# A three-layer fp32 block on one core: the order of work at its norm transitions, its first loads, and its filler matmuls are changed

## The reference, cut to what matters

```
h = rms_norm(x); proj = h @ w_in                 # first layer: retention and a gated recurrence
x = x + mix @ w_out                              # "out"
h = rms_norm(x); up = h @ w_up                   # norm transition 0, feed-forward 1 (conv, gelu, product)
x = rms_norm(x + hidden @ w_down)                # norm_f
for l in range(2):                               # two layers of a second kind
    h = swiglu_ffn(rms_norm(x)); x = x + 0.5 * rms_norm(h)       # feed-forward A
    h = hybrid_mixer(rms_norm(x)); x = x + rms_norm(h)           # mixer
    h = swiglu_ffn(rms_norm(x)); x = x + 0.5 * rms_norm(h)       # feed-forward B
```

## Time and profile before

| | |
|---|---|
| median of 3 runs | 1520.59 us (1520.00 to 1520.68) |
| the profiled execution | 1520.84 us |
| its span in the trace | 1518.7 us |
| PE busy | 1482.9 us, 98% of the span |
| DVE busy, ACT busy | 970.2 us (64%), 712.4 us (47%) |
| granted TensorE clock, mean | 0.999 of full speed |
| first product of a weight unit begins | 19.26 us |

### The profile page before, as it was taken

One profiled execution on the slowest core, in us unless ns is written; L12 is line 12 of the kernel. 1 busy time (PEld: TensorE's weight loads), 2 busy tenths in 40 slices (PEclk: granted clock), 3 DMA queues, 4 the chain that ended last, 5 costly groups with the idle time before them and its releaser, 6 DMA issues. The chain is left out here.

```text
span 1518.7 us, 21963 instructions
## 1 busy us (share of the span) xinstructions
PE 1482.9 (98%) x9232; PEld 1300.2 (86%) x9232; DVE 970.2 (64%) x1195; ACT 712.4 (47%) x878; POOL 39.5 (3%) x50
## 2 busy tenths in 40 slices
PE   7999999999999999999999999999999999999998
PEld 6999999899988788888987888878888899878886
DVE  5767786587864656545876666456664568666644
ACT  4533863455543544445245444444444444454432
POOL 0000000000000000001010000000000010000000
PEclk9999999999999999999999999999999999999999
DMA  7635465566655566465323755547655543366542
GB/s 245 222 121 167 141 198 189 159 189 180 182 194 166 180 221 210 151 196 139 112 98 112 228 182 185 188 145 228 229 194 168 139 123 115 102 192 192 194 148 101
DMA packets 253461, 259.17 MB, mean 171 GB/s; under 512 B 26659, under 2 KB 217524, under 8 KB 253364
## 3 DMA queue, kind: packets, MB, share of 16 engines
q1 hardware_dynamic: 251424, 254.44, 52.8%
q10 hardware_dynamic: 1940, 3.33, 0.6%
HBM read 256.69 MB, written 1.05 MB: 170 GB/s over the span
## 5 line engine op out<-in xcount | busy, mean ns | idle before, releaser
L971 DVE TENSOR_TENSOR w_lo<-raw,w_hi 128x2048 fp32r<-128x2048 f32 (+1 forms) x240 | 545.3, 2274 | 335.7 <-ACT w_hi L589 335.5
L589 ACT ACTIVATE w_hi<-raw 128x2048 fp32r<-128x2048 f32 (+1 forms) x240 | 455.9, 1900 | 345.3 <-PE stream L1634 145.4
L1634 PE MATMUL stream<-a_hi,w_hi 128*128 128x256 f32 x1072 | 306.4, 286 | 4.3 <-DVE a_lo L1008 3.2
L1634 PE MATMUL stream<-a_lo,w_hi 128*128 128x256 f32 x1072 | 303.3, 283 | 0.0
L1634 PE MATMUL stream<-a_hi,w_lo 128*128 128x256 f32 x1072 | 303.2, 283 | 0.0
L1634 PE MATMUL stream<-w_hi,a_hi 128*128 128x512 f32 (+1 forms) x640 | 244.0, 381 | 6.4 <-DVE w_lo L971 6.4
L1634 PE MATMUL stream<-w_hi,a_lo 128*128 128x512 f32 (+1 forms) x640 | 239.3, 374 | 0.0
L1634 PE MATMUL stream<-w_lo,a_hi 128*128 128x512 f32 (+1 forms) x640 | 238.9, 373 | 0.0
L1634 PEld LDWEIGHTS stream<-a_hi,w_hi 128*128 128x128 f32 x1072 | 205.6, 192 | 7.5 <-DVE w_lo L971 3.9
L1634 PEld LDWEIGHTS stream<-a_lo,w_hi 128*128 128x128 f32 x1072 | 205.7, 192 | 0.0
L1634 PEld LDWEIGHTS stream<-a_hi,w_lo 128*128 128x128 f32 x1072 | 205.6, 192 | 0.0
(11 more groups left out here) (282 smaller groups left out, 1612.0 us busy)
## 6 DMA issues: line engine op xcount, KB each, us to landing
raw<-in_ffn_w_up SPq DMA_DIRECT2D x136, 512.0 KB, 5.0
raw<-in_ffn_w_down SPq DMA_DIRECT2D x104, 512.0 KB, 4.5
raw<-in_ffn_w_gate SPq DMA_DIRECT2D x88, 512.0 KB, 3.9
raw<-in_w_in SPq DMA_DIRECT2D x78, 512.0 KB, 4.6
raw<-in_w_out SPq DMA_DIRECT2D x24, 512.0 KB, 4.2
raw<-in_w_ret_o SPq DMA_DIRECT2D x8, 512.0 KB, 4.1
raw<-in_w_lru_o SPq DMA_DIRECT2D x8, 512.0 KB, 4.0
diag<-in_conv_diag SPq DMA_DIRECT2D x8, 512.0 KB, 5.8
```

The source lines that it names most:

```text
L589: nc.scalar.activation(w_hi[s][:, :, 0:n], raw[s][:, :, 0:n], ACT.Copy).then_inc(w_hi_ready, 1)
L971: V.tensor_tensor(w_lo[s][:, :, 0:n], raw[s][:, :, 0:n], w_hi[s][:, :, 0:n].bitcast(F32), ALU.subtract).then_inc(w_split, 1)
L1634: return nc.tensor.matmul(dst, lhs, rhs, start=start, stop=stop, skip_group_check=True)
```

## The change

1. Roots: POOL takes post 0, post 1, pre 0, pre 1. To match, `next_variance` for tile 0 moves behind the post work of tile 1 on DVE, and (except into a mixer) `x_square` for tile 0 moves behind the third `hi` on ACT.
2. Splits: at transition 0, `turned_hi` for t = 1 moves ahead of `hi(U1_UP + 2)`, and `lo(U1_UP + 1)` and `lo(U1_UP + 2)` move behind `turned_lo` for t = 1. Into a mixer, `lo(last + 2)` and `lo(last + 3)` move behind `turned_lo` and the second `next_variance`, and `hi(last + 3)` behind the second `x_square`.
3. Gate transposes of pair 0 move behind the pass of unit 3, t = 0.
4. Loads: unit 0 is filled by SP; units 1 and 2 are filled only once the unit before has landed. The three small loads on ACT move behind `hi(0)`.
5. Fills: 22 and 4 become 14 and 1; 5 and 4 become 1 and 1; 19 and 4 become 11 and 1.

```diff
-    return 4 + 4 * (i - 1) + (t if i == NORMS - 1 else 2 * t + (not post))
+    return 4 + 4 * (i - 1) + t + 2 * (not post)
...
                 if c >= NS:
                     sp.wait_ge(w_split, c - NS + 1)
-                for dst, src in halves(raw[s]) if c else ():
+                elif c:
+                    sp.wait_ge(raw_loaded[c - 1], 32)
+                for dst, src in halves(raw[s]):
...
-                for t in range(TT):
-                    if post:
-                        inverse_root(rs4[:, t:t + 1], var4[:, t:t + 1], 1)
-                    if pre:
-                        inverse_root(rs4[:, 2 + t:3 + t], var4[:, 2 + t:3 + t], 1)
+                for at in [0, 1] * post + [2, 3] * pre:
+                    inverse_root(rs4[:, at:at + 1], var4[:, at:at + 1], 1)
...
             act.dma_start(keep[:, 0:NFIRST], io["table"][:, 0:NFIRST]).then_inc(ident_loaded, 16)
-            for half in range(2):
-                act.dma_start(raw[0][:, 4 * half:4 * half + 4, :], ...).then_inc(raw_loaded[0], 16)
             act.dma_start(sq[:, 0:2, :].rearrange("p a b -> p (a b)"), io["vec_rows"]).then_inc(vecs_loaded, 16)
-            act.dma_start(pos_i, ...)       # and sink_row, w2aug: the three small loads
...
             hi(0)
+            act.dma_start(pos_i, ...)       # and sink_row, w2aug
...
             x_half_square(4, 1, 1)
+            turned_hi(N_UP1, 1, 0, V1["norm2"])
             hi(U1_UP + 2)
-            turned_hi(N_UP1, 1, 0, V1["norm2"])
...
             x_half_square(8, 1, 1)
+            hi(U1_END + 2)
             x_square(N_F, 0, 1 / 16)
-            hi(U1_END + 2)
             turned_hi(N_F, 1, 2, 0)
...
             # between, on ACT
                 y_square(last, 1, 1, scale)
+                to_mixer = group is not None and col
+                if not to_mixer:
+                    hi(last + 3)
                 if group is not None:
                     x_square(i, 0, next_scale)
-                hi(last + 3)
-                if group is not None:
                     turned_hi(i, 1, group, col)
                     x_square(i, 1, next_scale)
+                if to_mixer:
+                    hi(last + 3)
...
             # transition 0, on DVE
-            lo(U1_UP + 1)
             add_half(U1_OUT + 3, 1, 1)
             two_halves(2, 1, 4, RMS_EPS)
             scaled(1)
+            turned_lo(N_UP1, 1, 0, V1["norm2"])
+            lo(U1_UP + 1)
             lo(U1_UP + 2)
-            turned_lo(N_UP1, 1, 0, V1["norm2"])
...
             # between, on DVE
-                lo(last + 2)
-                if group is not None:
-                    next_variance(i, 0, next_eps)
+                to_mixer = group is not None and col
+                if not to_mixer:
+                    lo(last + 2)
                 two_halves(0, 1, squared + 4, 4 * RMS_EPS)
                 at[1].append(gained(1, 1, squared + 4))
                 residual(i, 1, at[1])
-                lo(last + 3)
+                if not to_mixer:
+                    lo(last + 3)
                 if group is not None:
+                    next_variance(i, 0, next_eps)
                     turned_lo(i, 1, group, col)
                     next_variance(i, 1, next_eps)
+                if to_mixer:
+                    lo(last + 2)
+                    lo(last + 3)
...
-                    if t == 1 and m == 0 and g:
+                    if (j, t) == (3, 0) or t == 1 and m == 0 and g > 1:
                         turn_hidden(f, g - 1)
```

More of the change, by code:

```diff
@@ L644, in _ @@
             act.dma_start(keep[:, 0:NFIRST], io["table"][:, 0:NFIRST]).then_inc(ident_loaded, 16)
-            for half in range(2):
-                act.dma_start(raw[0][:, 4 * half:4 * half + 4, :],
-                              io["w_in"][0, 512 * half:512 * half + 512, 0:UC].rearrange("(k p) n -> p k n", p=P)).then_inc(raw_loaded[0], 16)
             act.dma_start(sq[:, 0:2, :].rearrange("p a b -> p (a b)"), io["vec_rows"]).then_inc(vecs_loaded, 16)
-            act.dma_start(pos_i, io["positions"].broadcast_to([P, T])).then_inc(small_loaded, 16)
-            act.dma_start(sink_row[:, :], io["sink_row"]).then_inc(small_loaded, 16)
-            act.dma_start(w2aug[:, :, :].rearrange("p l n -> p (l n)"), io["gate2"]).then_inc(small_loaded, 16)
             act.wait_ge(x_loaded, 16)
@@ L658, in _ @@
             hi(0)
+            act.dma_start(pos_i, io["positions"].broadcast_to([P, T])).then_inc(small_loaded, 16)
+            act.dma_start(sink_row[:, :], io["sink_row"]).then_inc(small_loaded, 16)
+            act.dma_start(w2aug[:, :, :].rearrange("p l n -> p (l n)"), io["gate2"]).then_inc(small_loaded, 16)
             act.dma_start(masks_f32, io["masks"]).then_inc(late_loaded, 16)
@@ L1349, in _ @@
             add_half(U1_END - 1, 1, 1)
-            next_variance(N_F, 0, 4 * RMS_EPS)
             two_halves(0, 1, 8, RMS_EPS)
@@ L1353, in _ @@
             lo(U1_END + 2)
+            next_variance(N_F, 0, 4 * RMS_EPS)
             turned_lo(N_F, 1, 2, 0)
@@ L1615, in _ @@
                 at.append([gained(1, 0, squared + 3)])
-                next_variance(i, 0, 4 * RMS_EPS)
                 two_halves(0, 1, squared + 4, RMS_EPS)
@@ L1620, in _ @@
                 lo(last + 3)
+                next_variance(i, 0, 4 * RMS_EPS)
                 turned_lo(i, 1, group, 32)
@@ L1859, in _ @@
                 wide_pass(c, t, y_bank(t, n), b_hi, b_lo, range(4 * m, 4 * m + 4), m == 0, m == 1, out_ready)
-            spin(psm[:, 0, :], 22)
+            spin(psm[:, 0, :], 14)
             turn(N_UP1, 1, y_gain)
-            spin(psm[:, 2, :], 4)
+            spin(psm[:, 2, :], 1)
             for j in range(NF1):
@@ L1902, in ffn @@
                         if i == N_L:
-                            spin(psm[:, 0, :], 5)
+                            spin(psm[:, 0, :], 1)
                         turn(i - 1, 1, x_t)
                         if i == N_L:
-                            spin(psm[:, 2, :], 4)
-                    if t == 1 and m == 0 and g:
+                            spin(psm[:, 2, :], 1)
+                    if (j, t) == (3, 0) or t == 1 and m == 0 and g > 1:
                         turn_hidden(f, g - 1)
@@ L1915, in _ @@
                 ffn(c0, 2 * l, i, lambda: turn(i, 0, x_t))
-                spin(psm[:, 0, :], 19)
+                spin(psm[:, 0, :], 11)
                 turn(i, 1, x_t)
-                spin(psm[:, 2, :], 4)
+                spin(psm[:, 2, :], 1)
                 cm, gm = c0 + UL_MIX, g0
```

## The result

The changed kernel takes 1507.58 us (median of 4 runs, 1505.71 to 1508.94); the kernel before, on the same chip, 1520.62. The ratio is 0.9914, 95% interval 0.9901 to 0.9926. So it is faster, as forecast, by 0.9%, but it won 13.0 us where 18.25 were forecast, and 1507.58 lies outside the range 1500.9 to 1506.0. The profiled execution took 1508.94. The runs of the changed kernel differ by 3.2 us, those of the kernel before by 0.7.

The account below looks back on a forecast made before the run. PE, busy 98% of the span, bounds the kernel; only its idle time can be won. Terms 3.4 + 3.1 + 1.75 + 1.6 + 4.6 + 3.8 = 18.25 us gave 1502.4 us, range 1500.9 to 1506.0.

Parts of the forecast that it names:

- The mixers' term: Transitions into a mixer, twice: moved splits and reordered roots win 2.3 us each, 4.6 for two.
- The start's term: Start: unit 0 lands earlier and its split starts earlier; range 2.6 to 4.0 us, 3.4 taken.
- Norm_f: Behind norm_f: post root of t = 1 no longer waits for row square and pre root of t = 0; 1.75 us.
- the first product of the mixers: Transition into a mixer: the first unit runs from 697.0 instead of 700.0, 3.0 us won there.
- the three small ones: Into feed-forward B twice and A of the second layer once: pre root out of the way, 1.6 us for three.
- the gate transposes: First gate transposes of the four feed-forwards: a pass later, PE no longer waits for gated values; 3.8 us.
- Transition 0: Products after transition 0 begin at 287.7 instead of 290.75, as splits move behind the chain; 3.1 us.
- The clause on what is late next: Start: later landings have slack; unit 2 lands at 20.5 to 22.5 and may be 2 to 3 us late.
- Rival 1: The start gives nothing because landings are late in a chain; 1505.8 us, chance 0.07.
- Rival 2: Clock falls at one to three transitions with cut fills, 1.4 us a fall; 1503.8 to 1506.6, chance 0.10.
- Rival 3: Splits moved back are late, into a mixer and at transition 0; 2.6 us go, 1505.0, chance 0.07.
- Rival 4: Ring of three buffers: delayed fills make every unit of feed-forward 1 late; 1521 and more, chance 0.01.

Follow-up runs that it names:

- gate_only: Kernel before with only the gate transposes moved a pass later; 3.94 us gained against 3.8 expected.
- start_fill: Changed kernel with 21 instead of 14 fills at the start; 1504.6 us, profiled execution 1504.12.
- after_again: Changed kernel run once more without any edit; median 1506.42 us, profiled execution 1508.29.
- root_later: Changed kernel with the mixers' inverse-rms product between the second and third operand tile of unit 1; median 1506.68 us.
- root_first: Changed kernel with VectorE waiting for the second tile's pre root before the moved splits in both mixer transitions; median 1507.58 us.
- half_split: Changed kernel with 21 start fills, later inverse-rms product, unit 1's split halved around the turned operands, unit 2's behind the gate rows; 1501.29 us.
- start_back: Changed kernel with only the start's loads as in the kernel before; median 5.1 us longer than that of after_again.
- fills_cover: Changed kernel with transition fills fitted to its pauses (17 and 5, 1 and 6, 13 and 4); 1.1 us over the expected 1504.5.
- fills_back: Changed kernel with the fills of the three transitions as long as before; its median differs by 1.3 us from that of after_again.
- no_hold: start_fill with SyncE issuing units 1 to 3 at once, not waiting for the unit before; 0.27 us lower than start_fill.
- splits_back: start_fill with the mixer transitions' splits and cast where the kernel before had them; 6.1 us lost against start_fill.

## Why the prediction was right in sign and wrong in size

**The steps that failed.** Two terms of the sum, and one that it lacked. The mixers' term of 4.6 us measured 2.75: with DVE's small steps done at 704.0, "just when PE asks for them", it took the root that PE's product for them needs, on GpSimd, as free, and the moved split holds that root. The start's term of 3.4 us measured 2.23 ahead of transition 0: 0.54 short at the first product, and 0.63 lost to a fall of the clock that the prediction had dismissed. And it put all that lies within the mixers, behind their first units, at nothing without a reason, where a pause in the second mixer's scores and the low clock behind it took 3.40.

**Right.** Norm_f to 0.01 us, the first product of the mixers to 0.13, the three small ones to 0.12, the gate transposes (3.8 forecast, 4.2 in the table, 3.9 alone in gate_only). Transition 0 gave 2.75 (2.77 in start_fill) of 3.1: products begin 6.43 us behind PE's last product of the part (279.34, 285.77), and 6.1 were forecast. What is missing lies ahead of `a_hi`, which begins 2.0 us nearer to that product than before (4.76 instead of 6.75 behind it), not 2.3: the square that it waits for now stands behind the other half's on ACT.

**The start: the loads come as forecast, the size is 0.5 off in one execution, and 0.6 is lost behind it.** The term was 3.4. start_fill won 3.60 at the first product, after_again 3.25, the first profile 2.86. What differed is how long PE's small products ahead of `rb` and of the vectors took: 0.62 and 0.60 us in start_fill, 1.06 and 0.67 in after_again, 1.06 and 1.06 in the first profile. It goes with the time at which the trace's records of the granted clock begin, at the upper level: 9.40, 10.81 and 11.84 us (the windows view counts what lies ahead of the first record as 1.00). In all 14 profiles the four products ahead of `rb` took 0.62 to 0.70 us where that is by 9.83, 1.06 where it is 10.63 or later, and 0.83 to 0.94 in the three between. I infer that the clock was still at its lower level ahead of that record; the time of the rise differs from one execution to the next, so up to 0.7 us of the start's term is luck.

The clause on what is late next, which followed landings alone, failed: the first landings were in time, and unit 2's, at 23.5 instead of 20.5 to 22.5, moved no product. What came was the clock's fall from 18.7 to 22.1, for which I had looked only behind transitions. I had written down the very pause, "1.3 us at the start", and dismissed it by the 1.4 us at 822.40 which kept 1.00. As I read it, the comparison failed because the paced products that follow at the start leave PE idle too (the prediction had the pieces 0.42 us apart, and they come 0.73 apart), while behind 822.40 it was busy. Filling the pause alone kept the clock up. The Trainium skill, page "TensorE: Matmul & The Clock Gate", section "HAM oscillation — how this bites in real kernels", which the prediction cited and set aside, tells of pauses that let the clock fall. These rows agree with that, though its example is of longer waits than the 1.4 us here.

**The mixers: the term 2.3 each measured 1.33 and 1.42.** The forecast had PE wait 0.6 us for the split; the table's drop of 1.54 instead of 0.7 is the wait for the root (1.3 us). Where the root's product stands later (root_later), the drop is 0.66: the forecast of the split's own wait was right. I had taken the root at its price beside idle or PSUM-reading DVE work (0.53) and moved a split of two SBUF operands next to it. root_first shows that the split holds it, half_split that the hold lasts as long as the split. The Trainium skill, page "SBUF — State Buffer", section "Who interferes with whom", says that a VectorE instruction with two SBUF inputs and a GpSimd one that reads SBUF exclude each other, not one that only writes; the trace agrees on both, for a zero fill beside the next split took 0.53 us, as it does in the kernel before beside nothing:

```profile
696.11 2.27 DVE L970 TENSOR_TENSOR w_lo<-raw,w_hi 128x2048 fp32r<-128x2048 f32 x1
696.24 0.53 POOL L542 MEMSET s_gla<- 128x512 f32 x1 [2.64 <-DVE glr_t L1519]
```

**3.4 us in the second mixer, in no step and no rival.** 1.91 for the pause, 1.49 for the clock behind it. The clock fell behind the pauses of 1.83, 1.83 and 1.81 us and stayed up behind those of 1.56 and 1.40 (start_back, root_later). The pause comes with the place of PE's instructions: it is there in all five profiles whose count of instructions ahead of it is the changed kernel's, and gone with 28, 88 or 160 more (four to a fill). Its place in PE's list is fixed too: 15809 records of PE (products, weight loads and those of its sequencer) lie ahead of the pause in each of the five, and 10177 ahead of the one in fills_cover, which is 5632 fewer, 22 times 256. In every case PE's products went on 2.2 to 2.4 us behind the start of a 16 KB instruction transfer.

```
kernel (mixer)      transfer behind the    pause   products go on behind
                    scores' first product          the transfer's start
root_later (2)      0.33                   1.40    2.39
start_back (2)      0.64                   1.56    2.24
fills_cover (1)     0.70                   0.92    2.31
changed (2)         0.77                   1.83    2.38
after_again (2)     0.78                   1.83    2.37
root_first (2)      0.80                   1.81    2.32
before (2)          1.00                   none
fills_back (2)      1.22                   none
start_fill (2)      1.97                   none
```

The rows are for the later of a mixer's two bursts of scores. A transfer early in the burst does not bring the pause by itself: the first mixer of start_fill has one 0.96 us behind, the first burst of the first mixer of the kernel before one at 0.00, and neither pauses.

The Trainium skill, page "Advanced Engine Details and Errata", section "ISA Cache", has cache lines of 16 KB, 256 instructions, and 128 KB in all on TensorE. The size of the transfers and the distance of 22 times 256 agree with the line; how many lines PE has at hand no row shows. My reading is that PE ran through one line before the next had come, in or right behind a burst of 120 small products. It is not shown: the rows show transfer, pause, place and the 2.2 to 2.4 us, not which engine a transfer is for or what PE's fetch does inside. Why a transfer is late at this line and not at others, and why the pause's own length varies, is open.

**Rivals.** Rival 1 (late landings) did not occur: no_hold and the flat lead behind 24 us. Rival 2 (the clock falls at cut transitions) did not either, but was the right mechanism in the wrong places: at the start (0.6 us, where the rival priced a fall at 1.4) and behind the pause (1.5); splits_back shows what it does when a mixer's pauses grow. Rival 3 named the right steps, "DVE's second split holds the small steps", but what was held was on GpSimd, and by the first split. Rival 4 did not occur.

**The sum again.** 18.25, less 0.54 and 0.63 at the start, 0.35 at transition 0, 1.85 in the mixers, 3.40 in the scores, and 0.4 more from the gate transposes: 11.9, the profiled execution's gain. start_fill takes away the first two and the scores: 4.6, and 16.6 in its profile. The median gained 13.0, 1.1 more than the profiled execution; its other runs have no trace, and that they kept the clock up at one of the two places is only argued.

## What to carry to other kernels

Before moving a long SBUF-to-SBUF VectorE instruction, look at what GpSimd does in its new place: a tiny root on the critical chain grows to the length of the big instruction, and halving that instruction halves the hold. A fill that is cut or a pause that is moved must be judged with the work behind it, since paced products after a pause can let the clock fall where dense work after a pause of about the same length did not. Where a kernel has bursts of very small products, adding or removing even 28 instructions far ahead can put in or take out a pause of 1 to 2 us, so look at the profile of each variant there before a difference of that size is put down to the edit.

## What the runs showed of the hardware

- A GpSimd operation of 0.54 us on one column took 2.52 beside a VectorE 128x2048 subtraction of two SBUF operands (2.28), and 1.45 beside one of 128x1024 (1.21); a fill of zeros of 128x512 kept its 0.53.
- PE stopped 0.9 to 1.8 us within or right behind a burst of 32x64 products with no semaphore in the way, going on 2.2 to 2.4 us behind the start of a 16 KB instruction transfer. In six profiles these stops stand at one place of PE's instruction count, or a multiple of 256 from it.
- Four 128x128 float32 products took 1.06 us ahead of the trace's first record of the upper clock level and 0.62 to 0.70 behind it; the record began anywhere from 9.2 to 11.8 us in kernels with the same start.
- Weight units issued at once on one queue landed the first at 9.91 us, against 9.76 when each waited for the one before; the time was 0.27 us lower.
